# Seven expert passes write their outputs as rows to DRAM and fetch them per token, in place of scatter products

## The reference

```python
def moe_swiglu(h, router, w1, w3, w2):
    logits = (h @ router).astype(jnp.float32)
    top_v, top_i = lax.top_k(logits, TOP_K)          # TOP_K = 2
    probs = jax.nn.softmax(top_v, axis=-1)
    gate = jnp.sum(jax.nn.one_hot(top_i, N_EXPERTS) * probs[..., None], axis=-2)
    out = jnp.zeros(h.shape, jnp.float32)
    for e in range(N_EXPERTS):                        # w1, w3: 1024 x 2816, w2: 2816 x 1024
        out = out + gate[..., e:e + 1] * swiglu(h, w1[e], w3[e], w2[e])
    return out
```

## Time and profile before

| quantity | value |
|---|---|
| median of 3 runs | 2525.79 us (2524.97 to 2526.66) |
| profiled execution: its time / its span | 2525.26 us / 2523.5 us |
| PE busy, DVE busy, ACT busy, POOL busy | 98%, 51%, 24%, 0% |
| mean DMA rate over the span | 198 GB/s |
| mean granted TensorE clock | 0.998 of full speed |

### The profile page before, as it was taken

How to read it: one execution, slowest core, us unless ns; L and a number is a source line. 1 busy time by engine, 2 the same in 40 slices (tenths; PEclk the granted TensorE clock), 3 DMA queues, 4 the chain that set the end, 5 groups by cost and what they waited for, 6 DMA issues and landing times. The chain is left out here.

```text
span 2523.5 us, 102692 instructions
## 1 busy us (share of the span) xinstructions
PE 2472.1 (98%) x45930; PEld 2082.2 (83%) x45930; DVE 1287.4 (51%) x3311; ACT 609.7 (24%) x1798; POOL 0.2 (0%) x4
## 2 busy tenths in 40 slices
PE   9999999999999999999999999999999999999998
PEld 8987666666698999998766666678999999999997
DVE  7665666666686676666576666667211111111111
ACT  2233333433311100233333334421111111111111
POOL 0000000000000000000000000000000000000000
PEclk9999999999999999999999999999999999999999
DMA  6334442222343454333353222234899999999997
GB/s 247 110 135 160 145 137 87 82 83 79 99 152 135 152 179 144 121 139 132 118 168 128 84 79 76 83 113 160 344 353 387 391 366 378 398 371 365 397 376 274
DMA packets 146052, 500.26 MB, mean 198 GB/s; under 512 B 18784, under 2 KB 23520, under 8 KB 143360
## 3 DMA queue, kind: packets, MB, share of 16 engines
q1 hardware_dynamic: 145792, 496.43, 54.7%
HBM read 476.07 MB, written 20.29 MB: 197 GB/s over the span
## 5 line engine op out<-in xcount | busy, mean ns | idle before, releaser
L294 PE MATMUL psum<-hT,ring 128*64 128x144 f32 (+1 forms) x4568 | 458.8, 346 | 3.4 <-DVE hT L2410 1.7
L447 PE MATMUL psum<-work,ring 128*64 128x88 f32 x11264 | 434.8, 239 | 3.6 <-issue 3.6
L447 PEld LDWEIGHTS psum<-work,ring 128*64 128x64 f32 x11264 | 433.2, 136 | 6.1 <-issue 5.8
L294 PEld LDWEIGHTS psum<-hT,ring 128*64 128x64 f32 x4568 | 292.4, 137 | 98.4 <-issue 13.4
L2916 DVE TENSOR_TENSOR work<-psum,work 128x88 f32<-128x88 f32 x176 | 44.2, 251 | 367.5 <-PE psum L447 367.5
L2639 PE MATMUL psum<-work,proj 128*64 128x88 f32 x5632 | 223.6, 239 | 1.1 <-issue 0.9
L2639 PEld LDWEIGHTS psum<-work,proj 128*64 128x64 f32 x5632 | 218.2, 136 | 5.9 <-issue 5.7
L1756 ACT ACTIVATE work<-psum 128x256 f32<-128x256 f32 (+4 forms) x320 | 104.0, 362 | 349.7 <-PE psum L1667 84.7
L294 PE MATMUL psum<-y_ret,work 128*64 128x144 f32 x2400 | 156.2, 286 | 1.2 <-DVE y_ret L524 1.2
L294 PE MATMUL psum<-work 128*64 128x144 f32 (+4 forms) x2096 | 154.7, 282 | 0.7 <-DVE work L524 0.7
L294 PEld LDWEIGHTS psum<-y_ret,work 128*64 128x64 f32 x2400 | 148.7, 137 | 1.4 <-issue 1.4
(11 more groups left out here) (497 smaller groups left out, 3730.3 us busy)
## 6 DMA issues: line engine op xcount, KB each, us to landing
ring<-w_ff_dram SPq DMA_DIRECT2D x424, 512.0 KB, 6.4
ring<-w_mix_dram SPq DMA_DIRECT2D x256, 512.0 KB, 4.3
proj<-w_ff_dram SPq DMA_DIRECT2D x128, 512.0 KB, 5.3
proj<-w_ff_dram SPq DMA_DIRECT2D x64, 384.0 KB, 5.5
work<-s_gla_dram SPq DMA_DIRECT2D x8, 1024.0 KB, 5.1
gla_s_out<-work SPq DMA_DIRECT2D x8, 1024.0 KB, 4.7
work<-s_ret_dram SPq DMA_DIRECT2D x8, 512.0 KB, 5.3
ret_s_out<-work SPq DMA_DIRECT2D x8, 512.0 KB, 3.0
```

Of the source, the lines that this page charges most:

```text
L294: last = nc.tensor.matmul(out[64 * c:64 * c + 64], weights[:, 64 * c:64 * c + 64], x, start=start, stop=stop)
L447: mm = nc.tensor.matmul(out[64 * c:64 * c + 64], ring[:, s, k, 64 * c:64 * c + 64], rhs[:, k0 + k, :], start=(k0 + k == 0), stop=(k0 + k = ...
```

## The change

Three edits.

1. **Expert passes.** The seven fixed passes no longer build `scatter` nor call `add_up`. Each block of outputs is transposed (`to_row`) and copied by ACT into a row buffer, `orow` (88 slots x 1024 features); after a pass POOL stores it to `expert_rows` in DRAM. After the seventh, POOL fetches for every token the rows of its two experts by six indirect transfers (a token whose expert is not among the seven reads a row of zeros), multiplies by the gates and adds. After the last pass TensorE transposes these sums to features (`rows_to_features`, 24 transposes) and DVE adds them to `xT` in three pieces. The down stage of a fixed pass is written out, eight blocks, where it was a loop of four turns. The eighth pass is as before.
2. **Retention.** DVE multiplies by the gate before `take_x(2)`, and by `rs` at the end.
3. **Start of GLA.** TensorE waits for two evacuations fewer (and for DVE's `taken`); DVE waits for the last evacuation only ahead of the last head's gate.

```diff
+                dve.wait_ge(sig("osq"), i + 1)
+                dve.wait_ge(sig("gate"), i + 1)
+                nc.vector.tensor_tensor(c1, o, gate, ALU.mult).then_inc(sig("on"), 1)
                 take_x(2)
                 take_y(2)
                 dve.wait_ge(sig("rs"), i + 1)
-                nc.vector.tensor_tensor(c1, o, rs, ALU.mult).then_inc(sig("on"), 1)
                 dve.wait_ge(sig("on"), i + 1)
-                dve.wait_ge(sig("gate"), i + 1)
-                nc.vector.tensor_tensor(y_ret[:, bass.ds(i * 2, 2), :], c1, gate,
+                nc.vector.tensor_tensor(y_ret[:, bass.ds(i * 2, 2), :], c1, rs,
                                         ALU.mult).then_inc(sig("y"), 1)
...
-            pe.wait_ge(retained("evac"), 6 + RET_H // 2 * 6)
+            pe.wait_ge(retained("evac"), 4 + RET_H // 2 * 6)
+            pe.wait_ge(retained("taken"), 1 + RET_H // 2 * 3)
...
+            def to_row(p, m):
+
+                if m == 0:
+                    pe.wait_ge(sig("hg"), count(p, 1, 2))
+                pe.wait_ge(sig("otok"), count(p, KT, m + 1))
+                pe.wait_ge(sig("oT"), count(p, KT, m + 3))
+                settle(pe)
+                nc.tensor.transpose(OTOK[m % 2][0:CAP, 0:128], oT[:, m % 2, :], ident).then_inc(sig("otok_ps"), 1)
...
+            def fixed_expert(p):
+
+                pe.wait_ge(sig("hg"), count(p, 1, 1))
+                settle(pe)
+                with pe.Fori(0, UP_SLABS // RING) as g:
+                    for n in range(RING):
+                        up(p, n, g)
+                for n in range(UP_SLABS // RING * RING, UP_SLABS):
+                    up(p, n, 0)
+                pe.wait_ge(sig("otok"), count(p, KT, 2))
+                gather_tokens(count(p, 1, 2))
+                pe.wait_ge(sig("w3_free"), count(p, FT, FT + 2))
+                settle(pe)
+                for m in range(KT):
+                    down(p, m // 2, m % 2)
+                    if m:
+                        to_row(p, m - 1)
+                to_row(p, KT - 1)
+
+            def rows_to_features():
+
+                pe.wait_ge(sig("weighed"), 3)
+                for n, (a, width) in enumerate(TILES):
+                    for k in range(KT):
+                        out = bank[4][:, NS * k:NS * k + NS] if n == 2 else bank[2 * n + k // 4][:, 128 * (k % 4):128 * (k % 4) + 128]
+                        last = nc.tensor.transpose(out, got[0][n][0:width, 128 * k:128 * k + 128], ident[0:width, 0:width])
+                    last.then_inc(sig("features"), 1)
...
             act.wait_ge(sig("added"), LAST + 2)
+            act.wait_ge(sig("whole"), 3)
...
+            for n, (a, width) in enumerate(TILES):
+                dve.wait_ge(sig("features"), n + 1)
+                ps = bank[4][:, 0:KT * NS] if n == 2 else psum[:, 1024 * n:1024 * n + 1024]
+                tt(xT[:, :, a:a + width], xT[:, :, a:a + width], ps.rearrange("p (k t) -> p k t", k=KT),
+                   ALU.add).then_inc(sig("whole"), 1)
...
+            for q in range(FIXED):
+                pool.wait_ge(sig("otok"), 2 + KT * (q + 1))
+                pool.dma_start(rows[CAP * q:CAP * q + CAP, :], orow).then_inc(sig("rowed"), 16)
+            pool.wait_ge(sig("rowed"), 16 * (FIXED + 1))
```

More of the change, by code:

```diff
@@ L1302, in norm @@
                 dve.wait_ge(sig("on"), i + 1)
+                if i == GLA_H - 1:
+                    dve.wait_ge(retained("evac"), 6 + RET_H // 2 * 6)
                 tt(y_gla[:, 2 * i:2 * i + 2, :], o, gate(i), ALU.mult).then_inc(sig("y"), 1)
@@ L2467, in experts @@
         lnv = w(T)
+        wheref, where = w(6), w(6).bitcast(U32)
+        orow, zero_row = flat(y_ret[:, :, :])[0:CAP, 0:D], flat(y_ret[:, :, :])[0:1, D:2 * D]
+        got = [[flat(t[:, :, :])[:, D * c:D * c + D] for t in (y_gla, merged, hT)] for c in range(2)]
+        rows = nc.dram_tensor("expert_rows", (FIXED * CAP + 1, D), F32).ap()
         sq = hid.rearrange("p f c -> p (f c)")[:, 0:4 * T].rearrange("p (n t) -> p n t", n=4)
@@ L2697, in _ @@
             with pe.Fori(0, FIXED) as i:
-                expert((i, 0))
+                fixed_expert((i, 0))
             rest = passes(pe)
@@ L2702, in _ @@
             LAST = rest * KT + FIXED * KT
+            pe.wait_ge(sig("otok"), LAST + 2)
+            settle(pe)
+            rows_to_features()
             for m in range(2):
@@ L2749, in expert, with take_row, fixed_expert @@
                     take_tokens(p, m + 1)
+            def take_row(p, m):
+                if m == 0:
+                    act.wait_ge(sig("rowed"), count(p, 16, 16))
+                act.wait_ge(sig("otok_ps"), count(p, KT, m + 1))
+                settle(act)
+                ac(orow[:, 128 * m:128 * m + 128], OTOK[m % 2][0:CAP, 0:128], cp).then_inc(sig("otok"), 1)
+            def fixed_expert(p):
+                nc.scalar.preload_act_table_set("silu_and_others")
+                for f in range(FT):
+                    silu(p, f)
+                nc.scalar.preload_act_table_set("natural_log_exp_and_others")
+                for m in range(KT):
+                    take_down(p, m)
+                    if m:
+                        take_row(p, m - 1)
+                take_row(p, KT - 1)
             def square(k):
@@ L2836, in _ @@
             tt(gather, gather, column_of(weight, CAP), ALU.mult).then_inc(sig("picked"), 1)
+            nc.vector.memset(zero_row, 0.0).then_inc(sig("zero_row"), 1)
             grant(dve, sig("w3_free"), sig("added"), by=2)
-            grant(dve, sig("scatter_ps"))
+            grant(dve, sig("scatter_ps"), by=1 + FIXED)
+            grant(dve, sig("gated"), by=FIXED)
+            grant(dve, sig("sc_ps"), sig("added"), by=FIXED * KT)
             nc.vector.memset(otok, 0.0)
@@ L2871, in _ @@
             then(tt(slot, slot, extra, ALU.add))
+            then(ts(wheref, flat(slot), float(FIXED * CAP), None, ALU.min))
+            copy(where, wheref).then_inc(sig("where"), 1)
             then(tt(before, rep(end, 1, MAXP), wide(cst("passno").unsqueeze(2), NE), ALU.is_le))
@@ L2907, in add_up, with expert @@
                 tt(xT[:, k, :], xT[:, k, :], ADD[m % 2][:, 0:T], ALU.add).then_inc(sig("added"), 1)
-            def expert(p):
+            def expert(p, fixed=False):
                 for f in range(FT):
@@ L2917, in expert @@
                        ALU.mult).then_inc(sig("w3_free"), 1)
-                    choose(p, f)
+                    if not (fixed and f == 4):
+                        choose(p, f)
                 take_gathered(count(p, 4, 4))
+                if fixed:
+                    return
                 for m in range(KT):
@@ L2923, in _ @@
             with dve.Fori(0, FIXED) as i:
-                expert((i, 0))
+                expert((i, 0), True)
             rest = passes(dve)
@@ L2928, in _ @@
             LAST = rest * KT + FIXED * KT
+            dve.wait_ge(sig("added"), LAST + 2)
+            settle(dve)
+            for n, (a, width) in enumerate(TILES):
[3 more added lines that the diff above has]
+                   ALU.add).then_inc(sig("whole"), 1)
+            dve.wait_ge(sig("whole"), 3)
             for m in range(2):
@@ L2936, in _ @@
                     op1=ALU.mult).then_inc(sig("normed"), 1)
+        @block.gpsimd
+        def _(pool):
+            pool.wait_ge(sig("zero_row"), 1)
+            pool.dma_start(rows[FIXED * CAP:FIXED * CAP + 1, :], zero_row).then_inc(sig("rowed"), 16)
+            for q in range(FIXED):
+                pool.wait_ge(sig("otok"), 2 + KT * (q + 1))
+                pool.dma_start(rows[CAP * q:CAP * q + CAP, :], orow).then_inc(sig("rowed"), 16)
+            pool.wait_ge(sig("rowed"), 16 * (FIXED + 1))
+            pool.wait_ge(sig("where"), 1)
+            for n, (a, width) in enumerate(TILES):
+                for c in range(2):
+                    nc.gpsimd.indirect_dma_start(
+                        got[c][n][0:width], None, rows[:, :],
+                        bass.IndirectOffsetOnAxis(where[0:width, 3 * c + n:3 * c + n + 1], 0)).then_inc(sig("got"), 16)
+            pool.wait_ge(sig("got"), 6 * 16)
+            gtt = nc.gpsimd.tensor_tensor
+            for n, (a, width) in enumerate(TILES):
+                for c in range(2):
+                    r = got[c][n][0:width]
+                    gtt(r, r, wide(gate2[0:width, c, n:n + 1], D), ALU.mult).then_inc(sig("where"), 1)
+                pool.wait_ge(sig("where"), 2 * n + 3)
+                gtt(got[0][n][0:width], got[0][n][0:width], got[1][n][0:width], ALU.add).then_inc(sig("weighed"), 1)
     def project_in(nc, block, sig, layer):
```

## The result

The changed kernel takes **2578.4 us** (median of four runs, 2577.9 to 2580.78) against 2525.38 us (2523.19 to 2526.66) before: a ratio of **1.0209, 95% interval 1.0195 to 1.0223**. It is slower by 53 us; 2566 had been forecast. The profiled execution took 2577.9 us, its span is 2575.9 us, 52.4 us more than the earlier trace rows.

What follows compares the result with a forecast made beforehand. TensorE's path was taken as the bound, with DMA 6.3 us under it per pass. Profiled 2525.3 + 39 (seven passes, 5.6 each) - 6 (retention, GLA) + 5 (pass 8) + 3 (end) = 2566 us, range 2502 to 2592.

Steps and rivals of the forecast that it cites:

- fetched again and in the way of the loads: Main case: each fixed pass refetches its longer code, delaying weight loads; 96.7 us a pass, 2566 us in all, chance 0.61.
- the second rival: Fixed passes: code fetched again without hurting the loads; about 90.7 us a pass, 2524 us in all; chance 0.08.
- Code, the number of fetches: Fixed passes: body of some 2,450 instructions not kept; 10 fetches of 16 KB a pass, about 60 to 70 more packets.
- Code, the cost of a fetch: Fixed passes: each fetch delays one part of the weight loads by 1.1 us; ten add 10.7 us a pass.
- The jump: End of each fixed pass: the jump back waits for its target, partly hidden under late loads; 0.3 us added.
- TensorE's saving: Fixed passes: without four `add_up` groups (3.9 us) and `scatter` transposes (0.5 us), 4.4 us less, 86.7 us a pass.
- the first rival: Fixed passes: the longer body is kept, saving 3 us a pass (2 to 4.4); 2506 us in all; chance 0.28.
- Waits in the down part: Down part of a fixed pass: 1 to 2 us of new waits, a `down_ring` slot being needed 1.3 us sooner.
- Retention and GLA: Before the expert passes: retention's waits for the second multiply go, -4 us; GLA's start -2 us; bounds 0 and -9.
- Pass 8: Last expert pass: six indirect transfers, 2.4 MB, 5.8 us at 408 GB/s, beside its loads; +5 us (0 to 6).
- POOL: Pass 8: nine multiplies and adds, at most 60 us, hidden under the pass; rival of POOL late, 2616 us, chance 0.03.
- The end: After the last pass: 24 transposes and DVE's three additions, the six squares now waiting for the last; +3 us (2 to 6).

Runs made afterwards that it cites:

- e2_long_before: The kernel before with only its down loop written out in the seven fixed passes, some 2,500 instructions, same work: 2592.95 us, ratio 1.0257.
- e8_kept_no_jump: The changed kernel with its down stage as four turns over two blocks, and TensorE's loop over the seven fixed passes written out: 2533.2 us, ratio 1.0027.
- e3_no_jump: The changed kernel with its seven fixed passes written out one after another on TensorE, no jump back between them: 2533.45 us, ratio 1.0024.
- e5_two_blocks: The changed kernel with a fixed pass's down stage as four turns of a loop over two blocks, some 1,370 instructions: 2526.83 us, ratio 1.0004.
- e4_front_edits: The kernel before with only the edits in retention and at the start of GLA: 2518.95 us, ratio 0.9972.
- e6_fill_36: The kernel before with 36 idle matmuls (144 instructions) at the end of each fixed pass, a body of some 1,510: 2552.49 us, one run.

## Why the prediction came out as it did

The sign was right, and the size fairly near (+41 us forecast, +53 measured): the body isn't kept. But the forecast's case was "fetched again and in the way of the loads", and only its first half is true; in mechanism the second rival, which left the loads unhurt and had a chance of 0.08, is nearer, and it fails on the price of the jump (1 to 3 us). The sum inside a pass came near by luck: two large errors cancel.

- **Code, the number of fetches**: ten a pass were forecast, 60 to 70 packets in all; there were 70 more. Right, and e2_long_before shows that the length of the code alone does it.
- **Code, the cost of a fetch**: the term 10.7 us for ten fetches (1.1 each, "if all delay the same part") was mis-sized. e8_kept_no_jump gives 0.2 to 0.3 us each, and e3_no_jump has nearly ten in passes of 92.3 us. Two of the signs named for it failed: TensorE waited for no `ring` or `proj` load in passes 2 to 7, and the share of the weights' queue fell to 91.5% (99.5% before) as its rate fell to 355 GB/s, so it stood idle and wasn't crowded. The landing times of the earlier trace rows rose in a part where loads were late by themselves, and one fetch had been given the whole rise. Where it does cost, TensorE stands in the down part for its own instructions: at 2030.01 it waits 0.98 us inside the first block, whose slabs were issued from 1954.9 to 1961.2 and landed within 6.3 us, over 60 us before, so that wait can't be for weights. The later two (0.22 and 0.82) may be for either.
- **The jump**: 0.3 us forecast; it cost 6.2, and 1.9 more at the half clock behind it. This is the step that failed most. The row it was taken from, ACT's 0.72 us, is another engine's way into new code; in the same place TensorE stood 1.17 us before and 1.82 after. The fetches of the pause show in the instruction queue: none from 1961 to 1964 us, one in 1964 to 1965, one in 1968.0 to 1968.1, and TensorE goes on at 1968.1. A stream of code has its fetches run ahead; here they come some 3.2 us apart while TensorE does nothing. It looks like round trips one after the other, but what fills the time between the packets isn't shown.
- **TensorE's saving**: 4.4 us forecast. The down part has 1.8 us less work and `scatter` gave 0.3. Of `add_up`'s 3.9 us, half comes back: seven single transposes of 0.24 to 0.28 us stand on the chain, 1.7 us where four pairs were 1.4; two downs with their seams are 7.08 (7.01 for the first two) where they were 6.91 (6.76), 0.8 in all; the last two downs, each with a stop inside, are 3.8 for 3.5, 0.6 more; and ahead of a pass's last transpose TensorE waits 0.4 us for ACT's copy. Had the body been kept, the saving forecast would have needed this order in a loop; in the order that fits, e5_two_blocks, it is 0.5 us a pass. So where the body was kept the time was 2527 us and not the first rival's 2506.
- **Waits in the down part**: 1 to 2 us forecast, 2.0 measured, though mostly for code and not for `proj`.
- **Retention and GLA**: -6 forecast, the passes began 5.4 us earlier, and e4_front_edits gives 7.5 by its medians. Right; the mechanism too, with GLA worth somewhat more: in layer 0 its first product starts at 230.42 us for 235.27, 2.5 us of which it had before GLA began, and 4.35 us of the lead are left at 268 us: 1.9 for GLA, where 1 had been counted. Of what TensorE waited for ahead of L724, DVE's 4.1 us of the earlier trace rows are gone, and this is left:

```profile
  DVEq L273: 0.7, 2
```

- **Pass 8**: +5 (0 to 6) forecast, 8.4 measured. The 5.8 us of bytes fit; missing were a longer way into the loop's code (1.82 us for 1.17) and the clock after a stop, as e5_two_blocks shows it. How the rest divides isn't measured.
- **POOL**: at most 60 us for its nine operations and hidden, forecast; they take 18.6 us and end 57 us ahead of their reader (the first three; 2 x 1.9 and 2.4 us, the last three, of 32 partitions, the same):

```profile
2481.93 3.75 POOL L3041 TENSOR_TENSOR y_gla<-y_gla,work 128x1024 f32<-128x1024 f32 x2 [11.49 <-DMA hT<-expert_rows,work]
2485.76 2.44 POOL L3043 TENSOR_TENSOR y_gla<-y_gla 128x1024 f32<-128x1024 f32 x1
```

- **The end**: +3 forecast, 3.7 measured, and by the mechanism named: the sums wait for the squares, and these for DVE's three additions (chain of the changed kernel; before, the sums began at 2510.30, right behind the last product).

```profile
2558.12 1.08 PE psum L2701 x8
...
2559.23 2.69 DVE xT L3010 x3
...
2562.52 4.17 PE psum L2729 x16
```

Per pass, then: forecast -4.4 + 10.7 + 0.3, less the 1.0 us by which the DMA was under TensorE, 5.6; measured -2.1 of work, +2.0 of waits in the down part, +6.2 of pause, +1.9 of clock, 8.0. Open are the exact limit of what is kept, what fills the 6 us of a pause, why e5_two_blocks stands 0.7 us longer at the end of a pass, and whether a loop could hold the changed kernel's order (one block late) in a body that is kept.

## What to carry to other kernels

Count the instructions of a hardware loop's body before writing a part of it out: if the chip no longer keeps it, each turn pays a pause at its jump back, and the slow clock behind it: 8 us a pass here, where the edit with a short body saved 0.5. If code has to be long anyway, write out the outer loop too: straight code streamed at 0.2 to 0.35 us a fetch (e8_kept_no_jump, e3_no_jump), and most of the cost was the jump. Before counting the removal of TensorE work as a gain, look at what it covered: `add_up` stood over ACT's copy, and in a kept loop nine tenths of its time came back as waiting.

## What the runs showed of the hardware

- TensorE kept a loop body of some 1,510 instructions from turn to turn, fetched one of some 1,630 anew at three of six jumps, and those of 1,750 and 2,450 at every jump. The four sizes are counted, not read from the profile.
- A jump back to code no longer kept stopped TensorE for 5.3 to 7.3 us in loops of 1,750 to 2,450 instructions and for 4.3 to 4.9 in one of 1,630; in straight code a fetch cost 0.2 to 0.3 us (e8_kept_no_jump), and at most some 0.35 (e3_no_jump, 3.3 us over 9.3 fetches).
- A stop of 6.6 us was followed by some 4 us near the 1.2 GHz level (0.54 from 1968 to 1972), and stops of 1.96 and 2.61 us close together by 5.6 us at it (0.50 from 2432.4 to 2438). In e6_fill_36 slower matmuls also followed 2.4 us of small ones with no stop over 0.5 us, in four of six passes (0.65 from 1969.6 to 1974).
- GpSimd took 1.9 us for a product and 2.4 us for a sum of 1024 columns in float32, over 32 partitions as over 128.
